# Scores of the second rotary attention: one float32 matmul against three matmuls of high and low parts

## The reference

```python
q, k, v = jnp.split(h @ w_qkv, [Hq * d, Hq * d + Hkv * d], axis=-1)   # 16 query heads, 4 key heads, d = 64
q = apply_rope(q.reshape(B, S, Hq, d), cos, sin)
k = apply_rope(k.reshape(B, S, Hkv, d), cos, sin)
s = jnp.einsum('bnqhgd,bnchd->bnhgqc', q, kb).astype(jnp.float32) * (d ** -0.5)
s = jnp.where(mask, s, -jnp.inf)          # |i - j| <= 128
m = jnp.maximum(jnp.max(s, axis=-1, keepdims=True), sink)
e = jnp.exp(s - m)
pr = e / (jnp.sum(e, axis=-1, keepdims=True) + jnp.exp(sink - m))
o = pr @ v, then o @ w_o
```

## Time and profile before

| what | value |
|---|---|
| median of three runs | 1023.87 us |
| the profiled execution's own time | 1023.89 us |
| span of its trace | 1022.2 us |
| PE busy | 1014.2 us, 99% |
| PEld busy | 869.7 us, 85% |
| DVE busy | 776.0 us, 76% |
| ACT busy | 609.0 us, 60% |
| POOL busy | 40.8 us, 4% |
| share of PE in the chain that ended last | 98% |

### The profile page before, as it was taken

One profiled execution on the slowest core, in us unless ns is written; L12 is line 12 of the kernel. 1 busy time (PEld: TensorE's weight loads), 2 busy tenths in 40 slices (PEclk: granted clock), 3 DMA queues, 4 the chain that ended last, 5 costly groups with the idle time before them and its releaser, 6 DMA issues.

```text
span 1022.2 us, 15541 instructions
## 1 busy us (share of the span) xinstructions
PE 1014.2 (99%) x5901; PEld 869.7 (85%) x5901; DVE 776.0 (76%) x1085; ACT 609.0 (60%) x931; POOL 40.8 (4%) x75
## 2 busy tenths in 40 slices
PE   9999999999999999999999999999999999999997
PEld 7777888888888877788888888899899978888886
DVE  6987678987887887869988887866667667656654
ACT  6667756665657668667656566734454655444443
POOL 1000010000000000000000000500000000000000
PEclk9999999999999999999999999999999999999999
DMA  8733445655555541536665646555453356565541
GB/s 281 269 124 126 137 153 203 207 198 178 199 172 184 178 167 43 185 124 204 208 205 166 205 165 206 177 190 170 154 178 124 125 185 206 186 212 178 182 146 42
DMA packets 115631, 177.36 MB, mean 174 GB/s; under 512 B 3643, under 2 KB 86900, under 8 KB 115572
## 3 DMA queue, kind: packets, MB, share of 16 engines
q1 hardware_dynamic: 115108, 175.24, 51.6%
q10 hardware_dynamic: 464, 1.32, 0.4%
HBM read 175.49 MB, written 1.05 MB: 173 GB/s over the span
## 4 chain that ended last, share of the span: by engine, by line
PE 98%; DMA 0%; issue 0%; DVE 0%; SPq 0%; POOL 0%; ACT 0%; POOLq 0%; DVEq 0%
PE ps L2004 94%; PE ps L2109 1%; PE ps L2554 1%; PE ps L2155 1%; DMA h<-in_x 0%; PE ps L2306 0%; PE ps L2698 0%; PE ps L2629 0%; PE ps L2326 0%; PE ps L2179 0%; DVE h L1963 0%; SPq L438 0%; PE ps L2271 0%; ACT xn L1240 0%; DVE pp L1968 0%
## 5 line engine op out<-in xcount | busy, mean ns | idle before, releaser
L1274 DVE TENSOR_TENSOR wlo<-raw,whi 128x2048 fp32r<-128x2048 f32 x147 | 335.4, 2287 | 74.3 <-ACT whi L673 74.2
L2004 PE MATMUL ps<-xs,whi 128*128 128x512 f32 (+1 forms) x1536 | 336.0, 351 | 0.0
L2004 PEld LDWEIGHTS ps<-xs,whi 128*128 128x128 f32 x1536 | 267.3, 189 | 38.6 <-issue 1.4
L673 ACT ACTIVATE whi<-raw 128x2048 fp32r<-128x2048 f32 x147 | 279.2, 1909 | 34.3 <-PE ps L2004 23.4
L2004 PE MATMUL ps<-xs,wlo 128*128 128x256 f32 x1248 | 202.3, 283 | 0.0
L2004 PE MATMUL ps<-whi,xs 128*128 128x512 f32 (+1 forms) x576 | 177.9, 392 | 0.4 <-issue 0.4
L2004 PEld LDWEIGHTS ps<-xs,wlo 128*128 128x128 f32 x1248 | 175.2, 191 | 2.9
L2004 PE MATMUL ps<-whi,ohi 128*128 128x512 f32 (+1 forms) x370 | 126.0, 397 | 0.0
L2004 PEld LDWEIGHTS ps<-whi,xs 128*128 128x128 f32 x576 | 106.7, 188 | 21.6 <-issue 1.4
L2004 PE MATMUL ps<-whi,olo 128*128 128x512 f32 (+1 forms) x370 | 123.2, 389 | 0.0
L2004 PE MATMUL ps<-wlo,ohi 128*128 128x512 f32 (+1 forms) x370 | 123.0, 389 | 0.0
(11 more groups left out here) (199 smaller groups left out, 982.4 us busy)
## 6 DMA issues: line engine op xcount, KB each, us to landing
raw<-in_ffn_w_up SPq DMA_DIRECT2D x44, 1024.0 KB, 5.1
raw<-in_w_in SPq DMA_DIRECT2D x23, 1024.0 KB, 5.3
raw<-in_ffn_w_down SPq DMA_DIRECT2D x22, 1024.0 KB, 4.9
raw<-in_w_mlp_in SPq DMA_DIRECT2D x16, 1024.0 KB, 5.4
raw<-in_w_mlp_out SPq DMA_DIRECT2D x16, 1024.0 KB, 5.0
raw<-in_diff_w_qkv SPq DMA_DIRECT2D x10, 1024.0 KB, 6.2
raw<-in_ple_w_gate SPq DMA_DIRECT2D x8, 1024.0 KB, 4.9
raw<-in_swa_w_qkv SPq DMA_DIRECT2D x6, 1024.0 KB, 5.3
```

Of the source, the lines that this page charges most:

```text
L673: act.activation(whi[:, u % RING, :], raw[:, u % RAW, :], ACT.Copy).then_inc(hi_ready, 1)
L1274: dve.tensor_tensor(wlo[:, u % RING, :], raw[:, u % RAW, :], whi[:, u % RING, :].bitcast(F32), ALU.subtract).then_inc(lo_ready, 1)
L2004: return pe.matmul(o, l, r, start=start, stop=stop, skip_group_check=True)
```

## The change

The rotated, transposed and (for the queries) scaled values are no longer kept as float32. ACT writes the fp32r high part out of bank `TB` (`k1_high`, `q1_high`, counted in the new semaphore `qk_hi`), and DVE reads the bank a second time and writes the low part (`k1_low`, `q1_low`). It is then DVE, not ACT, that counts `t_free`. The parts lie in tiles that are free at that time: `phi`/`plo` for the keys, `ohi`/`olo` tiles 4 to 7 for the first eight query heads, `xhi`/`xlo` tiles 0 to 3 for the others. `scores1` issues three fp32r matmuls in place of each float32 one. On DVE the two `rope_mul` of chunk 5 are pulled apart, and the split of the unit that stood behind them as `ahead(u + 3)` is now two halves. On PE the transposes `1q10` and `1q11` stand ahead of `pv1` where they stood behind it; the ACT and DVE work on them moves inside the next blocks' steps.

```diff
+        q1hi = [ohi[:, 4:8, :], xhi[:, 0:4, :]]
+        q1lo = [olo[:, 4:8, :], xlo[:, 0:4, :]]
+        k1hi, k1lo = phi[:, 0:2, :], plo[:, 0:2, :]
 # ACT
-                copy_k(slice(0, 2), 0)
+                def k1_high(t):
+                    act.wait_ge(t_ready, tcount[0] + 1)
+                    act.activation(k1hi[:, :, t * P:(t + 1) * P], ps[:, TB, 0:2 * P].rearrange("p (a c) -> p a c", c=P),
+                                   ACT.Copy).then_inc(qk_hi, 1)
+                    tcount[0] += 1
+                def q1_high(first, t):
+                    act.wait_ge(t_ready, tcount[0] + 1)
+                    act.activation(q1hi[first // 4][:, :, t * P:(t + 1) * P], ps[:, TB, :].rearrange("p (a c) -> p a c", c=P),
+                                   ACT.Copy, scale=0.125).then_inc(qk_hi, 1)
+                    tcount[0] += 1
+                k1_high(0)
                 ahead(u + 2)
-                copy_k(slice(0, 2), 1)
-                ahead(u + 3)
+                k1_high(1)
+                split_half(2)
                 for t in range(T):
-                    copy_qs(slice(0, 4), t)
+                    q1_high(0, t)
                 split_half(2)
...
                         for n in (s + 2, s + 3):
                             swa_exp(n)
                             sink_exp(n)
+                            if n in (6, 8):
+                                q1_high(4, (s - 4) // 2)
...
                     swa_hi(s)
-                    if s in (4, 6):
-                        copy_qs(slice(4, 8), (s - 4) // 2)
 # DVE
+                def k1_low(t):
+                    dve.wait_ge(qk_hi, t + 1)
+                    cols = slice(t * P, (t + 1) * P)
+                    dve.tensor_tensor(k1lo[:, :, cols], ps[:, TB, 0:2 * P].rearrange("p (a c) -> p a c", c=P), k1hi[:, :, cols].bitcast(F32),
+                                      ALU.subtract).then_inc(t_free, 1)
+                def q1_low(first, t):
+                    dve.wait_ge(qk_hi, 3 + first // 2 + t)
+                    cols = slice(t * P, (t + 1) * P)
+                    dve.scalar_tensor_tensor(q1lo[first // 4][:, :, cols], ps[:, TB, :].rearrange("p (a c) -> p a c", c=P), 0.125,
+                                             q1hi[first // 4][:, :, cols].bitcast(F32), ALU.mult, ALU.subtract).then_inc(t_free, 1)
                 ahead(u + 1)
+                k1_low(0)
                 ahead(u + 2)
-                for t in range(T):
-                    rope_mul(5, t, "qkv1.1", u + 3, 2, 8)
+                k1_low(1)
+                rope_mul(5, 0, "qkv1.1", u + 3, 2, 8)
+                split_half()
+                q1_low(0, 0)
+                rope_mul(5, 1, "qkv1.1", u + 3, 2, 8)
+                split_half()
+                q1_low(0, 1)
...
-                ahead(u + 3)
                 swa_max(0)
                 swa_max(1)
...
                         swa_scale(s + 2)
+                        if s in (4, 6):
+                            q1_low(4, (s - 4) // 2)
                         swa_scale(s + 3)
 # PE, scores1
                     for j in range(2):
-                        for r in range(2):
-                            rows_ = slice(r * HD, (r + 1) * HD)
-                            mm(pair[r][:, j, :], qS[rows_, 4 * g + i + j, qt * P:(qt + 1) * P], kT[rows_, g, :], j == 0, False)
+                        for n, (q, k) in enumerate(((q1hi, k1hi), (q1hi, k1lo), (q1lo, k1hi))):
+                            for r in range(2):
+                                rows_ = slice(r * HD, (r + 1) * HD)
+                                mm(pair[r][:, j, :], q[g][rows_, i + j, qt * P:(qt + 1) * P], k[rows_, g, :], j + n == 0, False)
 # PE, the loop over pairs
                     piece1(s)
-                    pv1(s)
                     if s in (4, 6):
                         qk_T(6, "1q1", (s - 4) // 2, flat_tiles((s - 4) // 2, 4))
+                    pv1(s)
```

More of the change, by code:

```diff
@@ L263, in three_layer_kernel @@
         table_loaded = sem("table_loaded")
+        qk_hi = sem("qk_hi")
         vecs_loaded = sem("vecs_loaded")
```

## The result

The changed kernel takes 1026.59 us in the median of 15 executions (1025.10 to 1027.52), the kernel before 1023.85 us beside it (15 executions, 1023.45 to 1024.24). The ratio is 1.0023 with a 95% interval of 1.0017 to 1.0030: slower by 2.7 us in the medians. The ratio lies just beyond the 0.2% that count as a change here, but its interval begins under it.

A forecast was written before the change was run, and what follows sets the result against it. The prediction took TensorE (PE), busy 99% of the span, as the bound: +2.25 us wait for `1q01`, - 1.1 us scores, + 0 for the rest = +1.15 us on 1023.9, so 1025.0 us; range 1023.4 to 1027.2 us.

The forecast's parts named there:

- the rival on the clock: TensorE's clock falls after the 2.25 us wait and stays low 2 to 4 us, costing 1 to 2 us; chance 7%.
- The wait for `1q01`: PE waits for DVE's rotation of query tile 1, now behind `q1_low(0, 0)`, and loses 2.25 us (1.9 to 2.6).
- The scores: Six fp32r couples per pair take 0.92 us instead of 1.06, saving 1.1 us over eight pairs (0.3 to 2.7).
- The two rivals on the couples: Score matmuls: row halves run one after the other, 1030.7 us, 6%; or loads not hidden behind same-row matmuls, 1029.0 us, 5%.
- The hand-overs costed at nothing: Key hand-overs, DVE's work ahead of the first maximum, and the second query hand-overs: all hidden, together 0 us.
- The keys: ACT's `k1_high` costs nothing; DVE's `k1_low` (0.42 us each) is hidden, with 1.5 us to spare before PE asks.
- `q1_low(0, 1)` ahead of the first maximum: On DVE before `swa_max(0)`: shifts with the 2.25 us wait, adds nothing, hidden with nothing to spare.
- Pairs 4 and 6: Second query hand-overs, transposes moved ahead of `pv1`: no cost, DVE frees the bank 0.27 us before PE wants it.
- a failed margin: If the 0.27 us to spare on the bank at pairs 4 and 6 fails, 0.2 to 0.5 us for both together.
- The sum: Whole kernel: +2.25 (wait) - 1.1 (eight score pairs) + 0 (the rest) = +1.15 us, giving 1025.0 us.

The follow-up runs named there:

- again: The changed kernel run once more, nothing edited; 1026.66 us median of 11, four at 1025.24 to 1025.63 and seven at 1026.50 to 1026.97.
- wait_alone: Kernel before, float32 scores kept, with the changed kernel's DVE order, a stand-in subtraction and ACT's unit split in halves; 1027.77 us median of six.
- long_wait: Changed kernel with the low part of query tile 0 computed twice more ahead of `q1_low(0, 0)`; 1029.48 us median of five.
- deferred: Changed kernel with PE's transposes `1q01` moved behind `scores1(0)` and `q1_piece(0, 3)`, ACT and DVE work moved later to match; 1023.70 us (11 executions).
- halves_apart: deferred_early with each pair's score matmuls reordered, all three of row half 0 before all three of row half 1; 1023.46 us median of ten.
- deferred_early: deferred with the transposes `1q00` also moved ahead of `q1_piece(0, 1)`; 1023.25 us (11 executions), 0.65 us under the kernel before.

## Why the prediction was right or wrong, step by step

**The measured time lies in the range, but where a rival put it.** The prediction's likeliest case was 1025.0 us with the clock up; that is where six of fifteen executions are (1025.10 to 1025.44). The median is with the nine others, at 1026.59 us, inside the 1026.0 to 1027.0 us that the rival on the clock gave, at a chance of 7%. So the median is in the range only because the range took in that rival, and it stands there by a majority of nine to six: with two more executions in the lower group it would have been about 1025.4 us. That much is luck, in both directions. Of the chances, 75% lay on a change of under 0.2%; the ratio came out just over it, with an interval on both sides. The step that failed is the one sentence that a wait of 2.25 us "is shorter", namely than the 2.8 us after which the clock had fallen at the kernel's end. That one fall after 2.8 us is an upper bound of what it takes and no lower one; I used it as a lower one. The runs show that 2.1 us of idle time suffices in over half of the executions. The fall then comes after PE has resumed, so the idle time need not last until it: 1.2 us after in the profile of `again`, 0.1 us in that of `wait_alone`, 0.4 us in that of `long_wait`. From the end of the last matmul before the wait it is 3.3, 2.2 and 4.0 us, so the 2.8 us were no fixed delay either. The rival's price, 1 to 2 us, was sized rightly: 1.54 us over 32 matmuls.

**The wait for `1q01`** was forecast at 2.25 us from the order of DVE's list. The starts show 2.27 us, the waits 2.1 us. Its working holds link by link: DVE idle for 1.58 us ahead of `q1_low(0, 0)`, released by ACT,

```profile
367.08 0.69 DVE L1731 SCALAR_TENSOR_TENSOR olo<-ps,ohi 128x512 fp32r<-128x512 f32 x1 [1.58 <-ACT ohi L1044]
367.69 0.68 DVE L1418 TENSOR_TENSOR scr<-ps,cosr 128x512 f32<-128x512 f32 x1
```

and the subtraction of 512 columns, for which the trace of before had no row, holds DVE for the 0.61 us between the two starts (0.60 taken). wait_alone shows the wait by itself, deferred its absence.

**The scores** were forecast to save 0.14 us a pair; 1.06 - 0.91 = 0.15 us, 1.2 us in all against 1.1. The steps of 0.12 us came as taken from the 128-row matmuls, and the ends of 0.2 us stayed. The Trainium skill, "TensorEngine Tiling (Array Packing)", Key Properties, states that a change of tiling mode drains the TensorE; the trace is in line with it, with 0.22 and 0.21 us for the first and last step where the others take 0.12, but no run parts a drain from a load with nothing to hide behind.

**The two rivals on the couples** did not come. The halves run side by side, and more robustly than I had thought (halves_apart). Loads hide behind matmuls of the same rows: twelve loads, recorded at 0.19 us each, and twelve matmuls on the same two row groups fit into steps of 0.12 us a couple. By the rule of the Trainium skill, "TensorE: Matmul & The Clock Gate", Part 3, that loads overlap in-flight matmuls only when the row group differs, a pair would have taken some 1.4 us; this case disagrees with it.

**The hand-overs costed at nothing.** The keys: right, no wait. `q1_low(0, 1)` ahead of the first maximum: right, `swa_max(0)` starts at 371.82, 1.91 us behind the start of `1q01` (369.91), and before it was 1.91 us too (369.71 - 367.80). Pairs 4 and 6: nearly right; the bank was in time in the changed kernel, but `q1_high(4, 0)` put ACT off, and its copy of the PLE product came 0.2 us late. I had followed the bank and the scalings there, not `ple_proj`, which stands behind the moved instruction on ACT. Its 0.2 us are as large as the least that I gave for a failed margin, but it was another wait than the one I named.

**The sum** was +1.15 us; with the clock up it is 1025.26 (median of the six) - 1023.85 = +1.4 us: +2.27 - 1.2 + 0.2 = +1.3.

## What to carry to other kernels

Where one engine is busy 99% of the span, ask of each change in another engine's list what it now stands behind: an instruction that waits for the bound engine, put ahead of one that the bound engine waits for, makes a round trip that no busy share shows. Price an idle gap of TensorE beyond its length: with 0.7 us no execution lost more, with 2.1 us over half of them lost another 1.5 us, with 3.6 us all five did. When single times fall into two groups, look at the granted clock of each before explaining a median, and take a profile from each group, for a mean over the span can hide where the clock was down. And before mending such a gap with faster work, look for independent work to put in it; here the changed order was worth 3.3 us in the medians (deferred_early against the changed kernel, in different sets), the faster scores 1.2.

## What the runs showed of the hardware that was not expected

- After 2.1 us of idle time 21 of 32 executions were some 1.5 us longer than the others of the same kernels (9 of 15, 7 of 11, 5 of 6), and the two profiles from the longer ones show the granted clock fall to 0.50, where one from the shorter ones shows it at 1.00. In all three profiles with a fall (the third with 3.6 us of idle time) it did not come during the wait, but behind it, with PE at work again.
- With matmuls of zeros in the wait (36 of 128 columns in 2.18 us) none of 11 executions was in the longer group, and the profile has the clock at 1.00.
- Matmuls of different row halves ran side by side even when three of one half stood ahead of three of the other in the list: 0.92 us from the first score to the mask, 0.91 when they alternate.
